# Moving the place of the stage tensors in SBUF by 64 bytes per partition, in a float32 kernel of three transformer-like blocks

## The reference: what is computed

```python
for layer in range(2):
    mod = silu(c) @ ada_w[layer] + ada_b[layer]         # 9 shifts, scales and gates of width 1024
    x = x + 0.5 * gate0 * swiglu(h, ffn_w_in, ffn_w_down)      # F0 (layer 0), F2 (layer 1)
    y = diff_attention(h) if layer == 0 else hgrn2(h)          # QKV + WO, or HIN + HO
    x = x + gate1 * y
    x = x + 0.5 * gate2 * swiglu(h, ffn_w_in, ffn_w_down)      # F1, F3
# then a second block (P2 + OUT): one product with 22 kinds of columns,
# gated linear attention, top-k sparse attention, pooling; concat @ w_out; final norm
def swiglu(h, w_in, w_down):
    a, b = split(h @ w_in)                              # 1024 x 5632
    return (silu(a) * b) @ w_down                       # 2816 x 1024
```

## Time and profile before

| | |
|---|---|
| three runs, us | 2414.72, 2413.76, 2407.76 (median 2413.76) |
| the profiled execution: its own time, us | 2414.24 |
| its span from the first to the last instruction, us | 2412.6 |
| TensorE busy with matmuls | 2379.7 us, 99% of the span, 11034 matmuls |
| VectorE, ScalarE, GpSimd busy, us | 1273.3, 861.0, 202.5 |
| granted clock of TensorE, mean | 0.994 |
| HBM traffic over the span | 120 GB/s |

### The profile page before, as it was taken

One profiled execution on the slowest core, in us unless ns is written; L12 is line 12 of the kernel. 1 busy time (PEld: TensorE's weight loads), 2 busy tenths in 40 slices (PEclk: granted clock), 3 DMA queues, 4 the chain that ended last, 5 costly groups with the idle time before them and its releaser, 6 DMA issues.

```text
span 2412.6 us, 30397 instructions
## 1 busy us (share of the span) xinstructions
PE 2379.7 (99%) x11034; PEld 1906.3 (79%) x11034; DVE 1273.3 (53%) x1953; ACT 861.0 (36%) x1320; POOL 202.5 (8%) x337
## 2 busy tenths in 40 slices
PE   7999999999999999999999999999999999999998
PEld 5888888677788888888888888888888888867766
DVE  6886334455678873343333355555533333459654
ACT  4232223566543222242222243344422222344453
POOL 1212000000002110000000013331000000020200
PEclk9999999999999999999999999999999999999999
DMA  8899332321259973223333321212233333232211
GB/s 279 281 289 286 110 96 73 97 62 53 70 170 290 285 228 108 86 79 96 96 99 108 89 79 53 62 53 79 85 99 96 96 110 96 66 95 66 61 53 53
DMA packets 420385, 285.27 MB, mean 118 GB/s; under 512 B 22690, under 2 KB 397788, under 8 KB 420304
## 3 DMA queue, kind: packets, MB, share of 16 engines
q1 hardware_dynamic: 397888, 207.64, 29.8%
q0 software_dynamic: 20896, 73.80, 9.2%
q10 hardware_dynamic: 1520, 2.77, 0.3%
HBM read 281.85 MB, written 6.72 MB: 120 GB/s over the span
## 4 chain that ended last, share of the span: by engine, by line
PE 92%; DVE 3%; ACT 2%; DMA 1%; issue 1%; SPq 1%; POOL 0%; ACTq 0%; DVEq 0%; POOLq 0%
PE bank L685 13%; PE bank L687 13%; PE bank L686 13%; PE bank L860 7%; PE bank L862 7%; PE bank L861 7%; PE bank L1529 4%; PE bank L1531 4%; PE bank L1530 4%; PE bank L1556 2%; PE bank L720 2%; PE bank L722 2%; PE bank L721 2%; PE bank L1178 1%; PE bank L1151 1%; PE bank L700 1%
## 5 line engine op out<-in xcount | busy, mean ns | idle before, releaser
L641 DVE TENSOR_TENSOR w_lo<-raw,w_hi 128x1024 fp32r<-128x1024 f32 (+1 forms) x331 | 434.1, 1312 | 427.3 <-ACT w_hi L622 421.8
L622 ACT ACTIVATE w_hi<-raw 128x1024 fp32r<-128x1024 f32 (+1 forms) x331 | 369.7, 1117 | 482.5 <-PE bank L687 242.9
L685 PE MATMUL bank<-h_hi,w_hi 128*128 128x512 f32 x1344 | 523.0, 389 | 1.1 <-DVE w_lo L641 1.1
L687 PE MATMUL bank<-h_hi,w_lo 128*128 128x512 f32 x1344 | 522.8, 389 | 0.0
L686 PE MATMUL bank<-h_lo,w_hi 128*128 128x512 f32 x1344 | 522.8, 389 | 0.0
L685 PEld LDWEIGHTS bank<-h_hi,w_hi 128*128 128x128 f32 x1344 | 252.3, 188 | 54.3 <-DVE w_lo L641 2.0
L686 PEld LDWEIGHTS bank<-h_lo,w_hi 128*128 128x128 f32 x1344 | 252.3, 188 | 52.4
L687 PEld LDWEIGHTS bank<-h_hi,w_lo 128*128 128x128 f32 x1344 | 252.3, 188 | 52.1
L860 PE MATMUL bank<-g_hi,w_hi 128*128 128x512 f32 x704 | 277.8, 395 | 0.0
L862 PE MATMUL bank<-g_hi,w_lo 128*128 128x512 f32 x704 | 276.0, 392 | 0.0
L861 PE MATMUL bank<-g_lo,w_hi 128*128 128x512 f32 x704 | 273.2, 388 | 0.0
(11 more groups left out here) (420 smaller groups left out, 3020.5 us busy)
## 6 DMA issues: line engine op xcount, KB each, us to landing
raw<-in_ffn_w_in SPq DMA_DIRECT2D x176, 512.0 KB, 4.0
ada<-in_ada_w POOLq DMA_DIRECT2D x128, 512.0 KB, 5.0
raw<-in_ffn_w_down SPq DMA_DIRECT2D x64, 704.0 KB, 4.6
raw<-in_hgrn_w_in SPq DMA_DIRECT2D x32, 512.0 KB, 4.0
raw<-in_attn_w_qkv SPq DMA_DIRECT2D x24, 512.0 KB, 3.8
raw<-in_w_in SPq DMA_DIRECT2D x22, 512.0 KB, 3.8
ada_first<-in_ada_w SPq DMA_DIRECT2D x16, 512.0 KB, 10.7
bias_scratch<-bias_lines POOLq DMA_DIRECT2D x14, 320.0 KB, 9.0
```

What stands on the lines that cost most here:

```text
L622: line(nc.scalar.activation(w_place(n, 0, k * P)[0], raw[:, n % 4, 0:k * P], ACT.Copy), hi_ready)
L641: line(nc.vector.tensor_tensor(lo, raw[:, n % 4, 0:k * P], hi.bitcast(F32), ALU.subtract), lo_ready)
L685: nc.tensor.matmul(out_ap, wh, xh, start=(k == 0), stop=False)
L687: last = nc.tensor.matmul(out_ap, wl, xh, start=False, stop=end)
```

## The change

One declaration is added behind `gend`, outside the scopes. It takes 16 float32, 64 bytes, in every partition; nothing reads or writes it.

```diff
         eight = sb("eight", [P, 3, 8])
         gend = sb("gend", [P, 2, 8])
+        sb("stage_start", [P, 16])
```

## The result

The change made the kernel slower: 2425.85 us (median of 5 runs, 2422.94 to 2427.03) against 2413.22 us (5 runs, 2407.76 to 2414.72), a ratio of 1.0052 with a 95% interval of 1.0041 to 1.0063. The forecast was 2408.0 us, with a range up to 2416. The two profiled executions are 10.3 us apart (2424.55 and 2414.24 us); what follows is an account of these 10.3 us.

The account below looks back on a forecast made before the run. TensorE was taken to bound the kernel, its matmuls busy 2379.7 of 2412.6 us. Profiled 2414.24 - 5.83 + 0.05 = 2408.5 us; for the median, 2413.76 - 5.8 = 2408.0 us, range 2403 to 2416.

Parts of the forecast that it names:

- the matmuls named: Triples' matmuls moved onto a multiple of 128: down products 2112, HO 192, WO 192, OUT 96, together 2592.
- The pace that I gave them: Down products, HO, WO and OUT's `yg` tiles would take the `h` products' 226.67 ns per matmul, saving 5.8 us.
- The third rival: In the 2592 matmuls, the new distance between moving operand and weights is worse: 20 us more, 2434 us; chance 0.10.
- The chance for a loss: Whole kernel: 0.10 for slower by the distance; slower by over 0.3% got 0.08.
- The second rival: HIN and P2, after the heads' small matmuls: even pace reached sooner, up to 6.3 us less, 2404.9 us expected; chance 0.11.
- The wait for `ada_first`: DMA wait of 7.84 us at the start: taken as 0 change; the skill page's rule would give 0.5 us less.

Follow-up runs that it names:

- The map: Stage padding of 224, 32, 96, 160 or 128 bytes in place of the change's 64, for distances 32, 96, 160, 224, 192: 2423.41 to 2425.31 us, one run each.
- All64: 64 bytes declared ahead of `xT`, moving every tensor of the kernel before by 64 bytes with all distances kept: 2413.26 us in one run.

## Why the prediction was wrong

*What bounds, and which instructions are touched: right.* The time moved through the pace of the matmuls named: 2400 of the 2592 stand in the windows, with 10.4 us of the 10.3. The other engines' durations and the small float32 matmuls stayed, and the clock was 1.00 in all the windows. That these matmuls lie on the path was right too.

*The pace that I gave them: the step that failed.* "I take for them the pace of the `h` products, 226.67 ns, since those are the nearest rows in everything but the place; the saving is 2592 x 2.25 = 5.8 us." The two facts in the rows, 226.67 ns at a multiple of 128 and 228.92 ns at 64 behind one, were exact, and the reading "so the multiple of 128 makes the difference" was one of several that they allow. The weights had the same place in every row, so a place and a distance couldn't be told apart. One sign against a price by place did stand in the rows: the three lines of the down triple have 395, 392 and 388 ns, though their moving tiles all stand 64 behind a multiple of 128; the prediction took the mean of the three and passed over the difference. The runs put the distance in its stead: after the change it is 128 rather than 0, and the price of that is +4.4 ns per matmul, not -2.25. The saving of 5.8 us exists, but at 192 or 448 bytes, where 0.2% were measured.

*The third rival had the right quantity, and was given one tenth.* It had the distance between the two operands as what counts, and even the number 128; that it counts because TensorE reads both at once is its own argument, which no run shows. Its price was too high, 7.8 ns from an `h` tile of OUT where 4.4 came, so 20 us instead of 10.3, and it counted within 512 bytes where 256 is the length. I held against it that the weights' tiles step by 512 bytes "without a trace of it in any window". That argument excludes lengths above 512, such that they would show between tiles, and says nothing on 512 or less; it was used as if it spoke against the whole rival.

*The chance for a loss.* I gave 0.10 to the side that came, with one price. A change whose only mechanism is a distance that no row of before has can land anywhere on an unknown curve. The map shows how such a draw goes: of the seven other distances one is better than 64 and six are worse.

*The second rival* (the even pace elsewhere comes sooner) didn't show: in the groups of the changed kernel the products between HGRN's and the second block's heads have 394 ns on both lines, where the earlier trace rows had 395 and 397, under 2 us together over 448 triples, and the stretch with HGRN's heads, between F2's down product and HO, didn't get shorter for it (275.30 us where it was 274.94).

*The Trainium skill.* The page "SBUF — State Buffer" of the Trainium skill gives 16-byte lines as what reads are sensitive to ("Specifications (TRN2)"), and lists two independent read ports for TensorE, one for moving data and one for weights ("Who interferes with whom"). Taken as statements on the pace, which the page doesn't make of them itself, neither agrees with the runs: all places were multiples of 32, yet the pace spans 226.7 to 234.3 ns, and moving the weights alone took the pace of an unmoved `h` from 226.7 to 233.4.

*The wait for `ada_first`.* The prediction put it at 0 in its sum, beside an estimate of 0.5 us less. The row after the change has 0.39 us less than the 7.84 of the earlier trace rows:

```profile
19.88 7.45 DMA ada_first<-in_ada_w
```

All64, the only other kernel in which `ada_first` starts at a multiple of 256, has 7.40; the eleven other kernels that show this wait have 7.71 to 7.84. The loads' median time from issue to landing is 10.3 and 10.2 us in these two and 10.6 to 10.9 in all the rest. So the estimate was right in kind and near in size; it is too small to be seen in the time.

*What stays open.* Why the distance counts at all. Why the distance of 64 costs a third of the others, and holds its pace with the extra matmul ahead as without. The price there, 3 x 2.25 = 6.8 ns per triple, happens to equal that of a single off-level matmul (233.33 - 226.67 = 6.7), but it isn't one slow matmul beside two even ones: by the earlier trace rows it lies on the first and the third (395 and 392 ns, with 388 on the second). Nor was it tried whether the 256 bytes hold for other widths than 512 columns or other types. Of the plain float32 matmuls of the earlier trace rows, `ada_first` by `cact` had its distance changed and kept 592 ns; `at` by `av` kept 275 ns, but there both operands moved together, so it tests nothing.

## What to carry to other kernels

The pace of these matmuls followed the difference between the places of their two operands, and neither place by itself. So before padding a moving tensor, work out where the weights stand, and bring the two level (here modulo 256 bytes) rather than either to a round number. Where rows give a pace at two places only, and the other operand never moved, they show a difference and not its cause; a forecast should then give the unknown side more than a tenth. The check is cheap and needs no timing statistics: count the matmuls of a known stretch in a window and divide, which is good to 0.1 ns, where the whole time needed a dozen runs.

## What the runs showed of the hardware

- With the three-matmul products of this kernel (128x128 stationary, 128x512 moving, TensorE at 2.4 GHz), the pace is 226.67 ns with the operands level modulo 256 bytes, and 233.3 to 234.3 ns off level; 228.9 ns at a distance of 64.
- The same operands at the same places can have two steady paces, 228.9 and 233.5 ns, for a whole stretch of 528 matmuls; one small float32 matmul ahead of it (0.2 us) decided which. This was seen with `g_lo` alone 128 bytes off level, in one run of either kernel.
- VectorE's and ScalarE's 128x512 operations kept their durations within 2 ns when their operands moved by 64 bytes (689 and 633 ns).
- Sixteen loads of 512 KB into `ada_first` landed in a median of 10.2 and 10.3 us where it starts at a multiple of 256 bytes (two kernels), and in 10.6 to 10.9 us elsewhere (fourteen kernels).
